# Two transformer blocks on one core: other orders of events in the two mixers, and narrower waits for the modulation's rows

## The reference

```python
# first model, for l in (0, 1)
x = x + 0.5 * swiglu(rms_norm(x, ffn1_norm[l]), ...)          # 1024 -> 2816 -> 1024
h = rms_norm(x, mix_norm[l])                                  # mixer A
parts = split_in_proj(h @ w_in[l])
o = concatenate([neighborhood(...), diff(...), gqa_axial(...), dilated(...)])
x = x + o @ w_out[l]
x = x + 0.5 * swiglu(rms_norm(x, ffn2_norm[l]), ...)
# second model, for l in (0, 1); mod = silu(c) @ w_ada[l] + b_ada[l], six rows of 1024
h = rmsnorm(x, g_mix_pre[l]) * (1 + scale_a) + shift_a        # mixer B
x = x + gate_a * rmsnorm(hybrid_mixer(h, ...), g_mix_post[l])
h = rmsnorm(x, g_ffn_pre[l]) * (1 + scale_f) + shift_f
x = x + gate_f * rmsnorm(swiglu_2(h, ...), g_ffn_post[l])
```

## Time and profile before

| | us |
|---|---|
| median of 3 runs | 1728.39 |
| lowest, highest | 1727.28, 1730.26 |
| the profiled execution, its time | 1729.25 |
| its span, first to last instruction | 1727.4 |

### The profile page before, as it was taken

One profiled execution on the slowest core, in us unless ns is written; L12 is line 12 of the kernel. 1 busy time (PEld: TensorE's weight loads), 2 busy tenths in 40 slices (PEclk: granted clock), 3 DMA queues, 4 the chain that ended last, 5 costly groups with the idle time before them and its releaser, 6 DMA issues.

```text
span 1727.4 us, 22247 instructions
## 1 busy us (share of the span) xinstructions
PE 1651.9 (96%) x8104; PEld 1369.5 (79%) x8104; DVE 1195.8 (69%) x1833; ACT 932.6 (54%) x1789; POOL 105.3 (6%) x155
## 2 busy tenths in 40 slices
...
GB/s 320 268 282 278 198 110 125 89 263 264 263 244 210 271 271 268 210 98 135 86 263 264 265 223 155 120 98 106 217 189 193 164 165 62 110 135 219 195 177 67
DMA packets 100107, 329.87 MB, mean 191 GB/s; under 512 B 18800, under 2 KB 19312, under 8 KB 99488
## 3 DMA queue, kind: packets, MB, share of 16 engines
...
## 4 chain that ended last, share of the span: by engine, by line
PE 84%; DVE 8%; ACT 4%; issue 1%; POOL 1%; DMA 1%; SPq 0%; DVEq 0%; ACTq 0%; POOLq 0%
PE PS L819 26%; PE PS L821 25%; PE PS L820 25%; PE PS L973 2%; PE PS L885 2%; DVE Wl L1644 1%; ACT WK L1368 1%; DVE PTl L1840 1%; PE PS L993 1%; DVE st L1809 1%; PE PS L836 1%; DVE QTl L1644 1%; ACT Wh L1252 1%; DMA raw<-in_ffn 0%; POOL st L2138 0%
## 5 line engine op out<-in xcount | busy, mean ns | idle before, releaser
L1644 DVE TENSOR_TENSOR Wl<-raw,Wh 128x1024 fp32r<-128x1024 f32 (+1 forms) x316 | 370.8, 1205 | 42.7 <-ACT Wh L1252 41.5
L819 PE MATMUL PS<-Wh,Hh 128*128 128x512 f32 (+2 forms) x936 | 370.0, 395 | 9.5 <-DVE Hl L1707 3.6
L821 PE MATMUL PS<-Wh,Hl 128*128 128x512 f32 (+2 forms) x936 | 364.8, 390 | 0.0
L820 PE MATMUL PS<-Wl,Hh 128*128 128x512 f32 (+2 forms) x936 | 364.7, 390 | 0.0
L1252 ACT ACTIVATE Wh<-raw 128x1024 fp32r<-128x1024 f32 (+1 forms) x316 | 316.4, 1041 | 30.7 <-PE PS L821 15.4
L1644 DVE TENSOR_TENSOR QTl<-raw,QTh 128x1024 fp32r<-128x1024 f32 (+2 forms) x178 | 211.9, 1210 | 18.9 <-ACT QTh L1252 18.8
L819 PEld LDWEIGHTS PS<-Wh,Hh 128*128 128x128 f32 x936 | 178.3, 190 | 48.3 <-DVE WK L1740 4.1
L821 PEld LDWEIGHTS PS<-Wh,Hl 128*128 128x128 f32 x936 | 178.0, 190 | 36.3
L820 PEld LDWEIGHTS PS<-Wl,Hh 128*128 128x128 f32 x936 | 178.3, 191 | 33.9
L819 PE MATMUL PS<-QTh,Hh 128*128 128x512 f32 (+2 forms) x504 | 197.3, 391 | 6.9 <-DVE Hl L1707 6.9
L821 PE MATMUL PS<-QTh,Hl 128*128 128x512 f32 (+2 forms) x504 | 195.5, 388 | 0.0
...
## 6 DMA issues: line engine op xcount, KB each, us to landing
...
```

The source lines that it names most:

```text
L819: e.matmul(out_, xh, wh, start=start, stop=False)
L820: e.matmul(out_, xh, wl, start=False, stop=False)
L821: return e.matmul(out_, xl, wh, start=False, stop=stop)
L1644: ins = e.tensor_tensor(low(p)[:, 0:w], raw[p % RAW][:, 0:w], high(p)[:, 0:w].bitcast(f32), ALU.subtract)
```

## The change

Three things. The tables of both mixers are written in another order for PE, ACT and DVE; the same events are in them, and POOL's are unchanged. SP's hook "a" moves from the stage's piece 6 to 8, its hook "bt" from 10 to 12. And the hook "b" waits for the writes of its own layer's rows alone, 12 for layer 0 and 24 for layer 1, where both waited for 24 before; DVE's "fg" 0 of the first mixer B waits for all 24 in exchange, as it writes to GQ.

```diff
             "PE": [("proj", 0, 0, 0), ("proj", 1, 0, 0), mid[0], mid[1], ("proj", 0, 1, 0), ("proj", 1, 1, 0),
...
-                ("T", 4, 0, 0), ("O", 2, 0, 0), ("S", 6, 0, 0), ("V", 4, 0, 0), ("T", 5, 0, 0), ("wo", (1,), 0, 0),
+                ("T", 4, 0, 0), ("O", 2, 0, 0), ("wo", (1,), 0, 0), ("S", 6, 0, 0), ("V", 4, 0, 0), ("T", 5, 0, 0),
...
@@ -760,9 +760,9 @@
-                hooks[first["a", l] + 6] = ("a", l)
+                hooks[first["a", l] + 8] = ("a", l)
                 hooks[first["b", l] + 4] = ("b", l)
-                hooks[first["b", l] + 10] = ("bt", l)
+                hooks[first["b", l] + 12] = ("bt", l)
...
                 if what == "b":
-                    e.wait_ge(mod_out, 16 * 24)
+                    e.wait_ge(mod_out, 16 * ADA_G * (l + 1))
...
@@ -1981,6 +1981,9 @@
                 if x == 0:
+                    if l == 0:
+
+                        e.wait_ge(mod_out, 16 * 2 * ADA_G)
                     e.wait_ge(j_act, act_steps(stage, 0, 1))
```

More of the change, by code:

```diff
@@ L129, in walk @@
                 ("wo", (1,), 0, 0), ("wo", (2,), 0, 0), ("wo", (3,), 0, 0), ("V", 6, 0, 0), ("S", 9, 0, 0), ("T", 7, 0, 0),
[2 rows of a table removed]
-                ("sums", 1, 0, 0), ("wo", (2,), 1, 0), ("wo", (3,), 1, 0), nxt[0], ("wo", (4,), 1, 0), ("rows", 1, 0, 0),
[2 rows of a table added]
+                ("wo", (6, 7), 0, 0), ("sums", 1, 0, 0), ("wo", (3,), 1, 0), nxt[0], ("wo", (4,), 1, 0), ("rows", 1, 0, 0),
                 ("wo", (5,), 1, 0), nxt[1], ("wo", (6, 7), 1, 0)],
-            "ACT": [("parts", 9, 0, 0), mid[0], ("proj", 0, 0, 0), ("parts", 10, 0, 0), mid[1], ("proj", 1, 0, 0),
-                ("parts", 12, 0, 0), ("proj", 0, 1, 0), ("parts", 12, 0, 0), ("norm", 0, 0, 0), ("parts", 14, 0, 0),
+            "ACT": [("proj", 0, 0, 0), ("parts", 8, 0, 0), mid[0], mid[1], ("parts", 9, 0, 0), ("proj", 1, 0, 0),
+                ("parts", 11, 0, 0), ("parts", 12, 0, 0), ("proj", 0, 1, 0), ("parts", 14, 0, 0), ("norm", 0, 0, 0),
@@ L136, in walk @@
                 ("proj", 1, 1, 0), ("norm", 1, 0, 0), ("proj", 2, 0, 0), ("turn_qk", 0, 0, 0), ("proj", 2, 1, 0),
-                ("parts", 18, 0, 0), ("E", 0, 0, 0), ("parts", 18, 0, 0), ("turn_qk", 1, 0, 0), ("proj", 3, 0, 0),
[3 rows of a table removed]
-                ("proj", 4, 1, 0), ("turn_qk", 2, 0, 0), ("norm", 3, 0, 0), ("parts", 28, 0, 0), ("N", 3, 0, 0),
-                ("E", 4, 0, 0), ("T", 3, 0, 0), ("V", 2, 0, 0), ("proj", 5, 0, 0), ("N", 4, 0, 0), ("V", 3, 0, 0),
-                ("T", 4, 0, 0), ("E", 5, 0, 0), ("parts", 28, 0, 0), ("proj", 5, 1, 0), ("parts", 30, 0, 0),
[4 rows of a table removed]
@@ new lines, in walk @@
+                ("parts", 17, 0, 0), ("turn_qk", 1, 0, 0), ("E", 0, 0, 0), ("proj", 3, 0, 0), ("N", 0, 0, 0), ("T", 0, 0, 0),
+                ("parts", 18, 0, 0), ("E", 1, 0, 0), ("parts", 19, 0, 0), ("parts", 21, 0, 0), ("N", 1, 0, 0),
+                ("proj", 3, 1, 0), ("norm", 2, 0, 0), ("parts", 24, 0, 0), ("T", 1, 0, 0), ("E", 2, 0, 0), ("N", 2, 0, 0),
+                ("V", 0, 0, 0), ("proj", 4, 0, 0), ("E", 3, 0, 0), ("T", 2, 0, 0), ("V", 1, 0, 0), ("parts", 25, 0, 0),
+                ("turn_qk", 2, 0, 0), ("proj", 4, 1, 0), ("parts", 28, 0, 0), ("norm", 3, 0, 0), ("V", 2, 0, 0),
[6 rows of a table added]
```

51 lines of the change are left out of this document (25 added, 26 removed), and 77 rows, old and new, of the table got.

## The result

The changed kernel takes 1707.52 us (median of 4 executions, 1706.23 to 1709.45), the kernel before, run beside it, 1728.89 (1727.28 to 1730.26). The ratio is 0.9879, with a 95% interval of 0.9864 to 0.9893: 21.4 us less, 1.2%. A second set of four executions of the changed kernel, with its own runs of before beside it (experiment r1), gave 1705.43 against 1729.83. The forecast was 1710, with a range of 1703 to 1723.

What follows compares the result with a forecast made beforehand. PE was taken as the bound, busy 1651.9 of 1727.4 us, leaving only its idle or slow moments to win. The terms 5.1 + 14.0 + 0 = 19.1 us off 1729.25 gave 1710.2, forecast 1710, range 1703 to 1723.

Steps and rivals of the forecast that it cites:

- part 1: SP's wait ahead of the first mixer B: with the narrower wait it becomes like the second, 5.1 us less.
- part 2: The new order in mixer B: 7.0 us less in each, 14.0 for both.
- part 3: The new order in mixer A: gains and losses cancel, 0; bounds 2.5 gained and 3.5 lost per mixer.
- Part 2b: Middle of mixer B: chunk 1 between O2 and S6 separates two waits, the clock stays up, 4.3 us per mixer.
- the prediction's first rival: Mixer B: half clock could follow from small 128-wide matmuls or begin at another wait; sum 7.3, 1722 us, chance 0.24.
- Part 2a: Mixer B's T1: its wait for ACT's half of N1 goes, 0.4 us gained per mixer.
- Part 2c: End of mixer B: O5's and wo 7.0's waits and half clock go, V7 gets 0.9; net 2.3 us per mixer.
- wo 5.0, 6.0 and 0.1 stand ahead and cover both waits: End of mixer B: these output chunks hide O5's 1.11 us wait and wo 7.0's 0.54.
- the forecast with mixer A's gain: The lower end of the range for 8 in 10, given as 1703 us; mixer A's bound was 2.5 gained per mixer.
- the clock in mixer B does not come back: Mixer B's half clock stays: 1.1 us per mixer instead of 7.0, sum 7.3, 1722 us; chance 0.24.
- rival of the slower side: DVE's queue in mixer A: late work makes S4, V3 and T4 wait together, half clock follows; 1733 us, chance 0.05.
- a chance of one half for 4.3 us each: Mixer B: if a half-clock stretch is only a sample, 4.3 us less gain for both mixers together, 1714 us.

Runs made afterwards that it cites:

- e1: The kernel before with only the narrower wait of SP's hook b and DVE's wait at fg 0, tables and hooks as before: 1722.40 us, ratio 0.9962.
- e2: The kernel before with only mixer B's new tables and hook "bt" at 12, the wait for all 24 writes kept: 1719.48 us, ratio 0.9943.
- e3: The kernel before with only mixer A's new tables and hook "a" at 8: 1722.93 us, ratio 0.9966.
- e4: The changed kernel with output chunk 1 of mixer B back behind T5, ahead of O3: 1714.19 us.
- e5: The changed kernel with PE's order behind T7 of mixer B as it was before: 1706.31 us.
- e7: The changed kernel with PE's order behind T8 of mixer A as it was, rows 0 and V9 next to each other: 1709.75 us.
- c1: The changed kernel with norm 0 of mixer A ahead of two weight pieces on ACT and one on DVE, as before: 1706.83 us.
- c4: c1 with mixer B's output chunk 5 back between T7 and V7, O5 staying where the change put it: 1705.44 us.
- e6: The changed kernel with T3 of mixer A back ahead of projection 5.0 on PE, other engines as changed: 1716.01 us.
- c2: The changed kernel with DVE's order in mixer A altered: turn_qk 2 ahead of N3, S4 and V2 ahead of the last weight piece and norm 3: 1714.88 us.
- c3: c2 with DVE's norm 3 ahead of V2 and T3, T4 ahead of rope 3, the last pieces behind rope 3: 1712.19 us.

## Why the prediction was right, and where only in its sum

| term | forecast | alone (e1, e2, e3) | other evidence |
|---|---|---|---|
| part 1, SP's wait | 5.1 | 6.5 | 4.65 by the traced step; PE's wait 4.01 to 1.36 |
| part 2, mixer B | 14.0 | 9.5 | chunk 1: 6.7 to 8.8 (e4) against 8.6; tail: 0.9 or nothing (e5) against 4.6 |
| part 3, mixer A | 0 | 6.0 | in e3's trace busy time 5.3 in the first, idle time 2.0 in the second |
| sum | 19.1 | 22.0 | together 21.4 and 24.4 |

**Part 1** was right in its mechanism and nearly so in its size, 4.65 by the traced step. The second mixer B as a control was good for it. The remaining wait is 1.36 and not 0.92, and that is what the measured step lacks to 5.1; why it remains, no run shows.

**Part 2b**, the clock behind O2 and S6, was the boldest term and the best one: 4.3 for each mixer, 3.4 to 4.4 measured. Its reasoning, two short waits next to each other against the same waits six us apart, is borne out by 8 mixers of 8 against 0 of 20. That the place of chunk 1 decides is shown. That it does so by the nearness of the two waits is not: the same move breaks up a long run of narrow matmuls (T4, O2, S6, V4, T5), which the prediction's first rival named, and no run does the one without the other.

**Part 2a**, T1's 0.4, is not shown: the wait is gone in all traces with the new tables, but in e1's with the old ones too, and in three traces (changed, r1, e7) lq 0 waits for 0.6 in its place in the first mixer B.

**Part 2c**, the tail, failed: 2.3 in each mixer was forecast, e5 shows nothing. V7's 0.98 was foreseen to 0.1. The step that failed is "wo 5.0, 6.0 and 0.1 stand ahead and cover both waits": it moved chunk 7 of half 0 back and did not ask what waits for it. That is the post norm and then turn_x, 0.86 us late. It is the old question of what is late next, asked at O5 and not at the stage's end. And the 1.5 us of clock are not bound to that place: five of the six mixers B with all the old tables (before, e1, e3) have a stretch at half clock behind O5, but e5 has the waits of O5 and wo 7.0 and no such stretch behind them in either mixer.

**Part 2 as a whole** was 4.5 us too high by e2's median and 2.3 by the two windows of its trace; the tail, with 4.6, is the term that was too large. The clock as a whole was well judged. The forecast priced only the stretches behind S6 and wo 7.0, which left the 6.8 us behind V0 of each mixer B and a window near 0.97. With the changed tables 3.4 to 13.7 us are left in a mixer B, leaving out what follows SP's wait in e2, and the two windows in the changed kernel are at 0.99.

**Part 3** failed on the other side. S4 was foreseen at 1.8 and is 1.95, T3's wait went, S8 went to 2.0 instead of 1.6, V3 waits for 1.9 instead of 1; the idle time in the first mixer A then came out within 1.5 us of the forecast zero, and within 0.4 in e3. What is missing is a term: I priced the half clock of mixer B and not that of mixer A, where 10.2 us of it stood in the first mixer, in all three traces with the old tables (before, e1, e2). With the changed mixer A, or all but the changed, it was 0 to 6.8 in eight traces (changed, r1, e3, e4, e5, e7, c1, c4). Of the second mixer A, some 2 us of idle time were not foreseen either: the forecast took it for a copy of the first. Its clock went the other way, 6.8 to 13.7 us at half clock in six traces (changed, r1, e3, e4, e5, e7) against 3.4 to 6.8 in the three with the old tables; in the changed kernel's own trace the second mixer A is 1.4 us longer than before. Which of the moves in mixer A's tables brings the gain in the first, the runs do not settle: e6 undoes one of them, and makes new waits by it.

So the forecast of 1710 came within 3 us of the first median because 4.5 us too much in part 2 and 6.0 too little in part 3 nearly cancel, and that is luck. Two of the prediction's sums do not close either, by little: less the 0.9 us that it names, 1710.2 is 1709.3, and the forecast with mixer A's gain of 2.5 us twice is 1705, not 1703. The rival "the clock in mixer B does not come back" is dead by e4. The rival of the slower side did not happen, but what it warned of is real: e6, c2 and c3 are each some 5 to 10 us slower than the changed kernel by a permutation in mixer A. Its mechanism, waits that cluster with half clock behind them, is that of e6 (13.7 us at half clock in the first mixer A against 6.8, and 2.8 us more idle time). c2 is another case: one long wait, with 4.2 us more idle time and only 3.4 us at half clock there.

**Chance against place.** The rule of the Trainium skill (TensorE: Matmul & The Clock Gate, section on the HAM clock gate), that the look at PE's activity is free-running and another run of a kernel shows other cold matmuls, had been weighed at a chance of one half for 4.3 us each. These runs divide it. For the stretches behind V0, bulk 3 and V7 of mixer B and most of mixer A, it is borne out: they come and go with unchanged code, and 2.6 to 4.0 us of a mixer's length with them. For the pair O2 and S6 it is not the whole story: there the stretch came every time, only its length varied between 6.83 and 10.24.
